# No scatter of dense gates begins near the end of the projection stages; the held ones follow in the next stage

## The reference, cut to what matters

```python
def block(xb):                                   # 128 frames
    q = (xb @ peer_wq).reshape(128, 8, 2, 128)
    s = jnp.einsum('thcd,hckd->thck', q, peer_sub_keys)
    s1, i1 = lax.top_k(s[:, :, 0], 16)
    s2, i2 = lax.top_k(s[:, :, 1], 16)
    ...                                          # 256 pair sums, of which the best 16
    top_s, top_pos = lax.top_k(cand_s, 16)
    experts = jnp.take_along_axis(cand_i, top_pos, axis=-1)
    g = jax.nn.softmax(top_s, axis=-1)
    act = jax.nn.gelu(jnp.einsum('thkd,td->thk', peer_u[experts], xb), approximate=False)
    return jnp.einsum('thk,thkd->td', g * act, peer_v[experts])
...
h = layer_norm(ALPHA * x + merged @ w_out, ln1_g, ln1_b)
y = layer_norm(ALPHA * h + peer(h), ln2_g, ln2_b)
```

## Time and profile before

| | us |
|---|---|
| median of 3 runs | 3311.8 (3307.9 to 3316.0) |
| the profiled execution | 3311.94 |
| its span, first to last instruction | 3309.9 |
| PE busy | 2940.7 (89%) |
| DVE busy | 2370.5 (72%) |
| POOL busy | 1531.3 (46%) |
| mean granted TensorE clock | 0.940 of full speed |

### The profile page before, as it was taken

How to read it: one execution, slowest core, us unless ns; L and a number is a source line. 1 busy time by engine, 2 the same in 40 slices (tenths; PEclk the granted TensorE clock), 3 DMA queues, 4 the chain that set the end, 5 groups by cost and what they waited for, 6 DMA issues and landing times. The chain is left out here.

```text
span 3309.9 us, 35268 instructions
## 1 busy us (share of the span) xinstructions
PE 2940.7 (89%) x10203; PEld 1633.8 (49%) x10203; DVE 2370.5 (72%) x4746; ACT 1204.4 (36%) x2936; POOL 1531.3 (46%) x1115
## 2 busy tenths in 40 slices
PE   8988989776797898877788899999999999999995
PEld 5754655443444555434445555544445445544442
DVE  0021487797787877878768878788778788887788
ACT  0142233484733344874653422222222222322222
POOL 0000066675673577877888733333333323333231
PEclk9989999897798999998799999999999999999998
DMA  4566689878899999667699999999999999999996
GB/s 140 188 249 232 215 317 354 310 256 280 272 358 389 381 333 354 178 204 209 182 296 315 393 416 415 415 415 415 414 415 415 415 415 415 411 416 410 387 392 256
DMA packets 380849, 1095.82 MB, mean 331 GB/s; under 512 B 91536, under 2 KB 217712, under 8 KB 294512
## 3 DMA queue, kind: packets, MB, share of 16 engines
q0 software_dynamic: 161664, 741.74, 59.1%
q1 hardware_dynamic: 176416, 302.67, 25.8%
q10 hardware_dynamic: 42576, 49.17, 4.3%
HBM read 1030.66 MB, written 61.71 MB: 330 GB/s over the span
## 5 line engine op out<-in xcount | busy, mean ns | idle before, releaser
L470 POOL DMA_INDIRECT expert_rows<-in_experts,picked_index x525 | 636.9, 1213 | 835.6 <-DVE ff_sum L622 711.4
L490 POOL DMA_INDIRECT gates_by_expert<-dense_gate,gate_address x384 | 691.9, 1802 | 214.0 <-issue 113.2
L610 DVE SCALAR_TENSOR_TENSOR expert_rows<-expert_rows,h_tile 128x1024 f32<-128x1024 f32 x557 | 678.0, 1217 | 150.0 <-DMA expert_rows<-in_experts,picked_index 135.9
L622 DVE SCALAR_TENSOR_TENSOR ff_sum<-expert_rows,coefficients,ff_sum 128x1024 f32<-128x1024 f32 x557 | 712.8, 1280 | 30.4 <-ACT coefficients L572 29.8
L1868 PE MATMUL dense_out_ps<-dense_value_rows,dense_weights 128*128 128x512 f32 x1536 | 687.1, 597 | 19.1 <-DVE dense_weights L1944 11.7
L1879 PE MATMUL dense_act_ps<-dense_hT,key_columns 128*128 128x384 f32 x2048 | 689.0, 490 | 16.9 <-DMA key_columns<-in_key_columns 12.9
L1879 PEld LDWEIGHTS dense_act_ps<-dense_hT,key_columns 128*128 128x128 f32 x2048 | 385.7, 190 | 333.3 <-DMA key_columns<-in_key_columns 60.0
L1868 PEld LDWEIGHTS dense_out_ps<-dense_value_rows,dense_weights 128*128 128x128 f32 x1536 | 293.3, 192 | 368.3 <-issue 321.1
L894 PE MATMUL proj_ps<-xT,w_in_block 128*128 128x384 f32 (+1 forms) x1392 | 421.8, 466 | 26.2 <-PEq L1668 12.6
L566 ACT ACTIVATE activated<-dots 128x1 f32<-128x1 f32 (+1 forms) x629 | 126.0, 200 | 718.6 <-DVE expert_rows L610 539.6
L894 PEld LDWEIGHTS proj_ps<-xT,w_in_block 128*128 128x128 f32 x1392 | 268.0, 193 | 179.4 <-issue 32.2
(11 more groups left out here) (204 smaller groups left out, 2970.5 us busy)
## 6 DMA issues: line engine op xcount, KB each, us to landing
key_columns<-in_key_columns SPq DMA_DIRECT2D x128, 512.0 KB, 37.1
dense_value_rows<-in_experts SPq DMA_DIRECT2D x128, 512.0 KB, 36.0
gates_by_expert<-zeros POOLq DMA_DIRECT2D x12, 2048.0 KB, 22.1
wq_half<-in_peer_wq SPq DMA_DIRECT2D x48, 512.0 KB, 11.8
dense_gates<-gates_by_expert SPq DMA_DIRECT2D x128, 192.0 KB, 36.5
w_in_block<-in_w_in ACTq DMA_DIRECT2D x18, 1024.0 KB, 11.0
w_in_block<-in_w_in SPq DMA_DIRECT2D x18, 1024.0 KB, 8.3
w_out<-in_w_out SPq DMA_DIRECT2D x24, 512.0 KB, 7.6
```

Of the source, the lines that this page charges most:

```text
L470: pool.indirect_dma_start(to, None, self.a["experts"], bass.IndirectOffsetOnAxis(ap=index[:, k:k + 1], axis=0)).then_inc(got, 16)
L490: pool.indirect_dma_start(self.a["gates_by_expert"], bass.IndirectOffsetOnAxis(ap=self.flat[i][:, k:k + 1], axis=0), self.dgate[i][:, k:k ...
L610: dve.scalar_tensor_tensor(place, place, 1.0, self.h[n % 2][:], ALU.mult, ALU.mult, accum_out=self.dots[:, s % TOPK:s % TOPK + 1]).then_in ...
L622: dve.scalar_tensor_tensor(total, self.slots[self.slot_of[p]][:, D:2 * D], self.coef[:, y % TOPK:y % TOPK + 1], total, ALU.mult, ALU.add). ...
```

## The change

A stage whose name is project or mla_project is closing from 85 per cent of its events on. While it is closing no scatter is put to an event, and the credit goes on growing without its cap. The first event of the next stage is not closing: all credit that has gathered is spent there at once.

```diff
--- before.py
+++ after.py
@@ -188,6 +188,7 @@
     OWN_AFTER = 0.35
+    SCATTERS_UNTIL = 0.85
@@ -336,10 +337,11 @@
         for k, (block, i, e) in enumerate(points):
             credit += share[block] * work(e)
-            while waiting and credit >= 1:
+            closing = block[1] in ("project", "mla_project") and i >= self.SCATTERS_UNTIL * len(self.beside[block])
+            while waiting and credit >= 1 and not closing:
                 credit -= 1
                 self.scatter_at.setdefault(key(k), []).append(waiting.pop(0))
-            credit = min(credit, 1.0)
+            credit = credit if closing else min(credit, 1.0)
```

## The result

The change made the kernel slower by about a third of a per cent: the ratio of the times after to before is 1.0034, with a 95% interval from 1.0023 to 1.0045 (medians of 9 runs each, 3323.11 us after and 3314.07 before). On 3314 us that is +11.3 us, from +7.6 to +14.9. The prediction was 3320.5, or +8.7; the profiled execution after took 3322.06, its span 3320.3.

What follows compares the result with a forecast made beforehand. POOL's scatters and fetches matter only where another engine waits for them. Terms -4.8 + 8.6 - 0.6 + 0 + 5.5 + 0 = +8.7 us gave 3320.5 us, range 3309 to 3329.

Steps and rivals of the forecast that it cites:

- Part 1: End of group 1's project: the landing wait of scatter (8, 0) leaves it, ACT becomes last, -4.8 us.
- Part 2: Group 1's stick: six more scatters and (8, 0)'s landing wait delay the fetches of rows 54 and 70, +8.6 us.
- Part 3: Group 1's mla_project: one item fewer for POOL's sequencer to hand over before PE's next start, -0.6 us or nothing.
- 4, end of project, group 2: Eight scatters leave, but ACT sets this end: 0, a gain of at most 0.3 us and no loss.
- Part 5: Group 2's stick: eight more scatters ahead of the third fetch make row 218 late, +5.5 us (+5.3 to +6.0).
- Part 6: Group 2's mla_project and mla: idle POOL takes in the shift and POOL bounds mla, 0, at most 1.6 us gained.
- A: Displaced scatters are hidden in both sticks and the boundary gain stays: 3306.5 us, faster; chance 0.08.
- B: Only one of the two sticks' costs shows: about 3313.5 us, no change that can be told; chance 0.25.
- C: Burst scatters in both sticks cost more than the mean, deciding above 2.3 us each: 3326.5 us; chance 0.12.
- The Trainium skill's fit for the landing: Rows 70 and 218 in the sticks: 4.4 us for 1 MB would land each 1.1 us sooner, sum +6.5.

Runs made afterwards that it cites:

- c_before: The kernel before, unedited, run once more for a second profile; span 3309.3 us, one run, no ratio.
- e3: Against the kernel before, only scatter (8, 0) moves, from the end of group 1's project to stick's first event; ratio 0.9983.
- e2: The change in group 2 alone, group 1 as in the kernel before; ratio to before 1.0014.
- t70: The changed kernel with scatters stopped from 70 per cent of the closing stages' events instead of 85; ratio to the kernel before 1.0121.
- t92: The changed kernel with scatters stopped from 92 per cent of the closing stages' events instead of 85; ratio to the kernel before 0.9998.
- e8: e6 with one scatter fewer ahead of the fetches of rows 222 and 223 in group 2's stick; ratio to the kernel before 0.9967.
- e6: Against the kernel before, (8, 0) held from group 1's project, and (12, 0) with two behind it from its mla_project, to the next stage; ratio 0.9966.
- e4: Against the kernel before, six scatters leave group 1's project, the order moves on through stick and six stand in stick's last event; ratio 0.9995.
- e1: The change in group 1 alone, group 2 as in the kernel before; ratio to before 1.0006.
- e9: e6 with two scatters more ahead of the fetches of rows 222 and 223 in group 2's stick; ratio to the kernel before 0.9983.

## Why the prediction was right, by its steps

The time, the sign and the mechanism were right: a wait of one scatter left the end of project, and the burst made rows late in both sticks. Two terms were mis-sized and one, the loads of weights, was missing. By place, in us:

| part | forecast | measured | read from |
|---|---|---|---|
| 1, end of project, group 1 | -4.8 | -4.8 | ACT's idle time 5.15 to 0.34 |
| 2, stick, group 1 | +8.6 | +6.2 | DVE's waits for rows |
| 3, mla_project, group 1 | -0.6 | +2.1 | its length; +3.0 of it w_uq_swapped |
| 4, end of project, group 2 | 0 | 0 | ACT's idle time 0.32 in both |
| 5, stick, group 2 | +5.5 | +7.2 | DVE's waits for rows |
| 6, mla_project and mla, group 2 | 0 | -2.0 | their lengths, -4.0 and +2.0 |
| sum | +8.7 | +8.7 | |

The span grew by 10.4. The other 1.7 us are a balance of differences that no part covers: +1.7 ahead of group 1's project, +1.4 in that project (3.4 shorter as a stage, 4.8 less of ACT's wait), +1.3 in the two sticks beside the waits for rows, -2.4 from group 1's mla to group 2's project and about -0.2 from group 2's merge on. None is larger than what c_before shows between two profiles of one kernel.

The prediction's sum has two slips, neither of which matters. Row 70's landing, 737.8 + 1.56 + 4.54 = 743.9, is 4.0 us behind 739.94 and not 3.8; and 3320.5 is 8.7 above the median of 3311.8, while 8.7 above the profiled execution is 3320.6.

**Part 1.** Right. It is shown by the profile and by e3, which takes this wait away alone and is faster.

**Part 2.** The mechanism was right, the term 2.4 us too large. The step that failed is the landing wait of (8, 0): taken as 4.04, measured 2.26, below both of my bounds, 3.08 and 6.39. The 4.04 had a fetch of 0.99 us in it, which stood between the two scatters (POOL's own idle time there was 2.75), and in the burst none did. Three rows of one kind of wait did not bound the next one. The rest is 0.6 from the scatters' lengths. In all, row 54's fetch began 672.75 - 638.87 = 33.9 us into the stage, forecast 672.1 - 635.8 = 36.3. I had 7.5 of the stall at row 54 and the other 1.1 at row 70; it was 5.5 at row 54 and 0.7 at row 68, and row 70 had just enough lead. POOL made good 3.6 us of the shift between rows 54 and 70 (14.05 to 10.46), forecast 3.3, though in part at a place that I had not counted: the scatter that had waited 6.39 at 720.21 waited 3.9 after.

**Part 3.** The term itself came out, the sum for the place did not. (12, 0) again set the stage's end:

```profile
806.14 1.55 POOL L492 DMA_INDIRECT gates_by_expert<-dense_gate,gate_address  x1 [3.14 <-DMA gates_by_expert<-dense_gate,gate_address]
808.10 1.62 PE L1353 MATMUL score_ps<-mla_kT,mla_qT 96*128 96x384 f32 x2 [12.74 <-PEq L1131]
```

PE starts 1.96 us after it, where it was 2.40: 0.4 of the forecast 0.6, for one item fewer to hand over. But ACT's copy early in the stage came 3.0 us later for the load. What the shift of POOL's fetches does to transfers of other queues wasn't priced at all.

**Part 5.** Mis-sized by 1.7 us. The shift at row 198, whose fetch began at 1332.48 before, was as worked out: (1352.97 - 1311.59) - (1332.48 - 1307.37) = 16.3 us against 15.9 to 16.6, and its wait 5.5. But I took row 218 as the place that sets the loss with the same shift; there it had grown to (1473.38 - 1311.59) - (1451.13 - 1307.37) = 18.0, and the fetch itself took 1.73 us in place of 0.99, so another 1.66 came on top.

**Part 6.** Neither the value, 0, nor the bound, a gain of 1.6, held: it was 2.0. The stage before mla was 4.0 us shorter, 2.1 of it from the wait for w_uq_swapped, a term that the prediction did not have. The rest is near the 1.6 that I had allowed for the two scatters: in the three profiles in which scatters left this stage (after, e2, t70) it was 4.0 to 4.2 shorter than before, in the two that had the short wait without that (t92, e8) 2.3 and 2.6. mla gave 2.0 back. That it did so because POOL bounds it was argued and not shown; DVE's waits for rows there were 20.7 us, before 20.6.

**The rivals.** A (hidden) and B (one cost of two) are out by the waits in both sticks. C would have shown in scatters above 2.3 us with their gap: the 13 in group 2's burst stand between 1326.29 and 1352.97, 2.05 us each, where 2.07 was forecast, and the eight in group 1's took 2.15 each beside the landing wait, where 2.23 was.

The effect that C drew from the Trainium skill ("SBUF — State Buffer", the "DVE blocks DMA" trap), scatters that take longer beside DVE's work, shows in this trace all the same; the means that the forecast used already held it. In the burst five scatters took 2.03 us or more and eight 1.61 or less. One of each, with the DVE instruction under way when it began:

```profile
1331.27 1.28 DVE L624 SCALAR_TENSOR_TENSOR ff_sum<-expert_rows,coefficients,ff_sum 128x1024 f32<-128x1024 f32 x1
1331.94 2.03 POOL L492 DMA_INDIRECT gates_by_expert<-dense_gate,gate_address  x1 [0.31 <-issue]
...
1348.37 1.23 DVE L1107 SCALAR_TENSOR_TENSOR softplus<-log_weight_ps,abs_exp_ln 128x1024 f32<-128x1024 f32 x1
1349.26 1.55 POOL L492 DMA_INDIRECT gates_by_expert<-dense_gate,gate_address  x1 [0.30 <-issue]
```

In the profile before, of the scatters from 470 to 1895 us, the 117 that began with no DVE instruction over 0.5 us under way took 1.57 us on average (1.55 to 1.64). The 183 that began within the two expert-row instructions (lines 610 and 622) took 1.97 and 1.98, up to 2.66. The 17 that began within the softplus instruction (line 1105), which reads one input from PSUM, took 1.58. So a scatter costs about 0.4 us more beside the experts' work on DVE; whether the cause is the one that the Trainium skill gives, POOL kept from writing descriptors, was not tested.

The Trainium skill's fit for the landing ("DMA: Bandwidth & Descriptors", the anatomy of one DMA on the gpsimd path), 4.4 us from issue, is short of what the new waits show: 1.61 + 4.64 = 6.25 us for row 54, 1.79 + 4.67 = 6.46 for row 198.

The agreement of +8.7 with +8.7 is partly chance: part 2 was too large by 2.4, part 5 too small by 1.7, and 3 and 6 are off by 2.7 and 2.0 in opposite directions.

## What to carry to other kernels

Look at what an engine has queued ahead of a point where all meet. In this kernel a backlog on POOL cost such a point next to nothing (ACT idled 0.32 us at the end of group 2's project with and without the eight scatters, and one item fewer to hand over gave 0.4 at another); an item with a semaphore wait cost 4.8. So look for that item and move it alone: one scatter moved gave 5.6 us and three more another 4.0 of PE's idle time, while moving the seventeen lost 11. Before displacing a prefetch, take its lead less its landing time and divide by the price of what is put ahead: about that many are free, and each further one costs its whole length (here 1.85 us). Leave one or two spare: by this rule five were free at row 218, and four cost 1.6 us.

## What the hardware showed that was not expected

A load of weights issued by SP at a stage's start landed up to 4.5 us later when POOL's gathers of 1 MB were issued just ahead of it. In group 2: 1.36 us of wait with the last gather ended 5.2 us before the stage's start, 2.8 to 4.4 with 3.4, 5.84 with the gather ended at the start. In group 1, where no edit was made for it, the tie is looser: 1.2 us with the gather ended 5.5 us ahead (e6), 1.1 to 3.5 with about 3, 3.9 and 2.4 with about 1.5 (before, e4), 4.1 to 6.9 with it at the start. The wait of a scatter for the landing of its tile's last scatter was 2.2 to 2.3 us behind the burst in group 1's stick (after, e1, t70), where 12 us or more had passed since the last fetch, and 5.8 to 6.4 at another place of the same stage (before, c_before, e2, e3, e8, e9), where two fetches stood right ahead of the last scatter. That the fetches lengthen it was not tried, and the 2.9 to 3.1 at (12, 0), with one fetch right ahead, shows that they are not all of it.
